# Expert stage of a hybrid diffusion step: the next chunk's first gate products between up and down, the result copied by ScalarE alone, one low weight piece on GpSimd

## The reference, cut to what matters

```python
xs = t[tok].astype(w_gate.dtype)                  # token rows, sorted by expert
hid = jax.nn.silu(lax.ragged_dot(xs, w_gate, sizes)) * lax.ragged_dot(xs, w_up, sizes)
y = lax.ragged_dot(hid, w_down, sizes)
```

## Time and profile before

| | us |
|---|---|
| median of three runs | 2013.52 |
| the three runs | 2010.44, 2013.52, 2013.54 |
| span of the profiled execution | 2009.7 |
| PE busy in it | 1754.8 (87%) |
| DVE busy | 1291.0 (64%) |
| ACT busy | 964.7 (48%) |
| POOL busy | 200.3 (10%) |

### The profile page before, as it was taken

The page is one execution under the profiler, slowest core; times in us unless marked ns, Lnnn a source line. Parts: engine busy times, 40 slices in busy tenths (PEclk is TensorE's granted clock), DMA queues, the critical chain, the costliest instruction groups (busy, mean ns, idle before and its releaser), DMA issues. The chain is left out here.

```text
span 2009.7 us, 40310 instructions
## 1 busy us (share of the span) xinstructions
PE 1754.8 (87%) x15365; PEld 1445.7 (72%) x15366; DVE 1291.0 (64%) x1849; ACT 964.7 (48%) x1499; POOL 200.3 (10%) x261
## 2 busy tenths in 40 slices
PE   3998977899897799999949998999998959999992
PEld 0898677788754688888838886888884548888882
DVE  1488354556545796896664872656664379899674
ACT  2254522333322786885544454323342257888651
POOL 0000022212100100000020000212220000000001
PEclk7999999999898899999969999999998969999996
DMA  8221094331023798897663111433002079999854
GB/s 323 73 85 45 1 363 166 129 128 54 6 114 153 311 393 355 319 399 279 235 220 115 43 45 42 142 128 97 2 3 108 32 295 383 400 404 396 334 209 167
DMA packets 113582, 376.64 MB, mean 187 GB/s; under 512 B 15178, under 2 KB 35938, under 8 KB 87846
## 3 DMA queue, kind: packets, MB, share of 16 engines
q1 hardware_dynamic: 84782, 303.86, 40.0%
q10 hardware_dynamic: 20168, 39.89, 5.1%
q0 software_dynamic: 8496, 30.94, 4.2%
HBM read 332.87 MB, written 41.78 MB: 186 GB/s over the span
## 5 line engine op out<-in xcount | busy, mean ns | idle before, releaser
L2084 DVE TENSOR_TENSOR expert_w_lo<-shared,expert_w_hi 128x2048 fp32r<-128x2048 f32 x192 | 430.4, 2284 | 46.6 <-ACT expert_w_hi L2026 45.7
L2026 ACT ACTIVATE expert_w_hi<-shared 128x2048 fp32r<-128x2048 f32 x192 | 359.6, 1909 | 44.0 <-PEq L143 39.6
L1968 PE MATMUL ps<-expert_w_hi,expert_x_hi 128*128 128x512 f32 x592 | 231.9, 392 | 6.3 <-DVE expert_x_lo L2080 6.3
L1970 PE MATMUL ps<-expert_w_hi,expert_x_lo 128*128 128x512 f32 x592 | 231.5, 391 | 0.0
L1969 PE MATMUL ps<-expert_w_lo,expert_x_hi 128*128 128x512 f32 x592 | 231.4, 391 | 0.0
L1968 PEld LDWEIGHTS ps<-expert_w_hi,expert_x_hi 128*128 128x128 f32 x592 | 111.9, 189 | 30.4 <-issue 7.1
L1970 PEld LDWEIGHTS ps<-expert_w_hi,expert_x_lo 128*128 128x128 f32 x592 | 111.8, 189 | 23.4
L1969 PEld LDWEIGHTS ps<-expert_w_lo,expert_x_hi 128*128 128x128 f32 x592 | 111.9, 189 | 23.2
L2004 PE MATMUL ps<-expert_w_hi,expert_hid_hi 128*128 128x512 f32 x296 | 118.6, 401 | 2.0 <-ACT expert_hid_hi L2058 1.1
L1127 POOL TENSOR_TENSOR mixer_NTb<-mixer_Bt,consts_sb 128x256 f32<-128x256 f32 x120 | 88.3, 758 | 285.5 <-DVE mixer_Bt L1402 222.2
L2005 PE MATMUL ps<-expert_w_lo,expert_hid_hi 128*128 128x512 f32 x296 | 115.5, 390 | 0.0
(11 more groups left out here) (372 smaller groups left out, 3668.1 us busy)
## 6 DMA issues: line engine op xcount, KB each, us to landing
shared<-in_w_up SPq DMA_DIRECT2D x64, 1024.0 KB, 8.6
shared<-in_w_down SPq DMA_DIRECT2D x64, 1024.0 KB, 8.9
shared<-in_w_gate SPq DMA_DIRECT2D x64, 1024.0 KB, 7.2
qkv<-in_w_ada SPq DMA_DIRECT2D x20, 1280.0 KB, 6.3
shared<-in_w_in SPq DMA_DIRECT2D x10, 2048.0 KB, 8.1
y_table<-expert_y ACTq DMA_DIRECT2D x37, 512.0 KB, 8.7
qkvT<-in_w_ada SPq DMA_DIRECT2D x20, 768.0 KB, 8.6
y_table<-zero ACTq DMA_DIRECT2D x1, 12800.0 KB, 52.3
```

Of the source, the lines that this page charges most:

```text
L1968: pe.matmul(bank, hi, w_hi[:, j, w], start=first, stop=False)
L1970: return pe.matmul(bank, lo, w_hi[:, j, w], start=False, stop=last)
L2026: act.activation(w_hi[:, j, :], raw[:, j, :], ACT.Copy).then_inc(w_hi_done, 1)
L2084: dve.tensor_tensor(w_lo[:, j, :], raw[:, j, :], w_hi[:, j, :].bitcast(F32), ALU.subtract).then_inc(w_lo_done, 1)
```

## The change

In `expert_phase` alone:

- TensorE: a chunk now consists of the second half of its gate products, the 8 transposes of the next x, the up products, the first half of the next chunk's gate products (`gate_head`) with the hid transposes behind its second and third product, and down. The first `gate_head` stands ahead of all chunks. In the very last chunk of a layer the next chunk's parts are left out, its x transposes too.
- x_hi and x_lo are made in halves of 128 x 512 (`x_half`).
- ScalarE: piece 0 of the next w_hi comes ahead of silu; the order is warm, piece 0, silu, piece 1, first half of x_hi, piece 2, second half of x_hi, the hid halves, pieces 3 and 4, y, piece 5, y transfer. y is one copy of 128 x 1024 out of banks 5 and 6.
- VectorE: piece 0, first half of x_lo, hid, second half of x_lo, the low parts of hid, pieces 1 to 4. It copies no y.
- GpSimd: makes the low part of piece 5 (`split_last`), behind the gather; gathers are numbered one higher and one is issued ahead of the chunks.
- SyncE: waits for piece 5 on a semaphore of its own (`w_lo_last`).

The diff, cut to its core:

```diff
                     for j in range(PIECES):
-                        sp.wait_ge(w_lo_done, e * PIECES + (j + 1))
+                        if j < LP:
+                            sp.wait_ge(w_lo_done, e * LP + (j + 1))
+                        else:
+                            sp.wait_ge(w_lo_last, e + 1)
                         sp.dma_start(raw[:, j, :], piece_of(A, l, e + 1, j)).then_inc(raw_in[j], 16)
...
-                def gather_next(k):
-                    pool.wait_ge(xt_p, k + 2)
+                def gather(k):
+                    pool.wait_ge(xt_p, k + 1)
                     pool.sem_inc(passed, 1)
-                    pool.tensor_copy(cur[:, :], R.idx[:, bass.ds(k + 1, 1)]).then_inc(picked, 1)
-                    pool.wait_ge(picked, k + 1)
+                    pool.tensor_copy(cur[:, :], R.idx[:, bass.ds(k, 1)]).then_inc(picked, 1)
+                    pool.wait_ge(picked, k)
...
-                for_experts(pool, lambda e, k, last, final: gather_next(k))
+                def split_last(e):
+                    pool.wait_ge(w_hi_done, e * PIECES + PIECES)
+                    pool.tensor_tensor(w_lo[:, LP, :], raw[:, LP, :], w_hi[:, LP, :].bitcast(F32), ALU.subtract).then_inc(w_lo_last, 1)
+
+                def chunk(e, k, last, final):
+                    if not (last and final):
+                        gather(nc.s_assert_within(k + 2, 2, MAXC))
+                        if last:
+                            split_last(e + 1)
+
+                gather(1)
+                split_last(0)
+                for_experts(pool, chunk)
...
-                def product(bank, hi, lo, j, col, first, last):
-
-                    w = slice(col, col + 512)
-                    pe.matmul(bank, hi, w_hi[:, j, w], start=first, stop=False)
-                    pe.matmul(bank, hi, w_lo[:, j, w], start=False, stop=False)
-                    return pe.matmul(bank, lo, w_hi[:, j, w], start=False, stop=last)
+                def product(bank, q, j):
+
+                    w, at = slice(q % 4 * FF, q % 4 * FF + 512), slice(q * P, (q + 1) * P)
+                    pe.matmul(bank, x_hi[:, at], w_hi[:, j, w], start=(q == 0), stop=False)
+                    pe.matmul(bank, x_hi[:, at], w_lo[:, j, w], start=False, stop=False)
+                    return pe.matmul(bank, x_lo[:, at], w_hi[:, j, w], start=False, stop=(q == KD - 1))
+
+                def gate(q):
+                    return product(G.ps[:, 0, :], q, q // 4)
+
+                def up(q):
+                    return product(G.ps[:, 1, :], q, 2 + q // 4)
+
+                def gate_head(e, k, between):
+
+                    pe.wait_ge(x_lo_done, k * 2 + 1)
+                    pe.wait_ge(w_lo_done, e * LP + 1)
+                    for q in range(4):
+                        mm = gate(q)
+                        if q in between:
+                            between[q]()
+                    mm.then_inc(g_half, 1)
 
                 for s in (u_p, xt_p, ht_p, y_p):
                     pe.sem_inc(s, 1)
-                turn(0, 0, KD)
+                turn(0)
+                gate_head(0, 0, {})
 
                 def chunk(e, k, last, final):
-                    pe.wait_ge(x_lo_done, k + 1)
+                    pe.wait_ge(x_lo_done, k * 2 + 2)
+                    pe.wait_ge(w_lo_done, e * LP + 2)
+                    for q in range(4, KD):
+                        mm = gate(q)
+                    mm.then_inc(g_p, 1)
+                    if not (last and final):
+                        turn(k + 1)
                     pe.wait_ge(hid_done, k * 2 + 1)
-                    for n, done in ((0, g_p), (1, u_p)):
-                        for q in range(KD):
-                            j = 2 * n + q // 4
-                            if q % 4 == 0:
-                                pe.wait_ge(w_lo_done, e * PIECES + (j + 1))
-                            at = slice(q * P, (q + 1) * P)
-                            mm = product(G.ps[:, n, :], x_hi[:, at], x_lo[:, at], j, q % 4 * FF, q == 0, q == KD - 1)
-                            if last and q == 3:
-                                mm.then_inc(half_used, 1)
-                        mm.then_inc(done, 1)
-                    turn(k + 1, 0, 4)
-                    hid_turn(k, 0)
-                    turn(k + 1, 4, 6)
-                    hid_turn(k, 1)
-                    turn(k + 1, 6, KD)
-                    pe.wait_ge(ya, k + 1)
-                    pe.wait_ge(yd, k + 1)
+                    for q in range(KD):
+                        if q % 4 == 0:
+                            pe.wait_ge(w_lo_done, e * LP + (3 + q // 4))
+                        mm = up(q)
+                        if q % 4 == 3:
+                            mm.then_inc((u_half, u_p)[q // 4], 1)
+                    if last and final:
+                        hid_turn(k, 0)
+                        hid_turn(k, 1)
+                    else:
+                        pe.wait_ge(sg_done, k + 1)
+                        gate_head(e + 1 if last else e, k + 1, {1: lambda: hid_turn(k, 0), 2: lambda: hid_turn(k, 1)})
+                    pe.wait_ge(y_done, k + 1)
                     for q in range(KF):
                         j, at = 4 + q // 2, slice(q * P, (q + 1) * P)
-                        if q % 2 == 0:
-                            pe.wait_ge(w_lo_done, e * PIECES + (j + 1))
+                        if q == 0:
+                            pe.wait_ge(w_lo_done, e * LP + LP)
+                        if q == 2:
+                            pe.wait_ge(w_lo_last, e + 1)
...
-                def take(k):
-                    act.wait_ge(xt_p, k + 2)
-                    act.wait_ge(u_p, k + 1)
-                    act.activation(x_hi[:, :], turned, ACT.Copy).then_inc(x_hi_done, 1)
+                def take(m):
+                    act.activation(x_hi[:, x_half(m)], turned[:, x_half(m)], ACT.Copy).then_inc(x_hi_done, 1)
 
...
                 split(0)
                 act.wait_ge(xt_p, 2)
-                act.activation(x_hi[:, :], turned, ACT.Copy).then_inc(x_hi_done, 1)
+                for m in range(2):
+                    take(m)
                 for j in range(1, PIECES):
                     split(j)
 
...
 
                         if last and not final:
                             act.wait_ge(raw_in[j], e * 16 + 16)
-                            if j % 2 == 0:
-                                act.wait_ge(half_used, e * 3 + (j // 2 + 1))
-                            elif j < 5:
-                                act.wait_ge((g_p, u_p)[j // 2], k + (1 + j // 2))
-                            else:
-                                act.wait_ge(y_p, k * 2 + 3)
+                            act.wait_ge((g_half, g_p, u_half, u_p, d_half, y_p)[j], k + (1, 1, 1, 2, 1, 2)[j])
                             split(j)
 
                     act.activation(warm[:, :], G.eps[:, :], ACT.Silu)
+                    next_hi(0)
                     act.wait_ge(g_p, k + 1)
                     act.wait_ge(hid_done, k * 2 + 1)
                     act.activation(sg[:, :], G.ps[:, 0, :], ACT.Silu).then_inc(sg_done, 1)
-                    for j in range(3):
-                        next_hi(j)
-                    act.wait_ge(y_p, k * 2 + 1)
+                    next_hi(1)
+                    if not (last and final):
+                        act.wait_ge(xt_p, k + 3)
+                        act.wait_ge(u_half, k + 1)
+                        take(0)
+                    next_hi(2)
+                    if not (last and final):
+                        act.wait_ge(u_p, k + 2)
+                        take(1)
+                    act.wait_ge(y_p, k + 1)
                     for m in range(2):
                         act.wait_ge(ht_p, k * 2 + (m + 2))
                         act.activation(h_hi[:, m * HQ * P:(m + 1) * HQ * P], hid_turned(m), ACT.Copy).then_inc(h_hi_done, 1)
-                    take(k + 1)
                     next_hi(3)
                     next_hi(4)
-                    act.wait_ge(y_p, k * 2 + 3)
+                    act.wait_ge(y_p, k + 2)
                     act.wait_ge(y_out, k * 16 + 16)
-                    act.activation(y[:, 0:512], G.ps[:, 5, :], ACT.Copy).then_inc(ya, 1)
+                    act.activation(y[:, :], G.ps[:, 5:7, :].rearrange("p b n -> p (b n)"), ACT.Copy).then_inc(y_done, 1)
                     next_hi(5)
-                    act.wait_ge(ya, k + 2)
-                    act.wait_ge(yd, k + 2)
+                    act.wait_ge(y_done, k + 2)
...
-                def take(k):
-                    dve.wait_ge(x_hi_done, k + 1)
-                    dve.tensor_tensor(x_lo[:, :], turned, x_hi[:, :].bitcast(F32), ALU.subtract).then_inc(x_lo_done, 1)
+                def take(k, m):
+                    dve.wait_ge(x_hi_done, k * 2 + (m + 1))
+                    dve.tensor_tensor(x_lo[:, x_half(m)], turned[:, x_half(m)], x_hi[:, x_half(m)].bitcast(F32),
+                                      ALU.subtract).then_inc(x_lo_done, 1)
 
...
```

(33 more changed lines are left out.)

22 lines of the change are left out of this document (12 added, 10 removed).

## The result

The changed kernel takes 2069.36 us (median of 4 runs, 2067.23 to 2078.41) where the kernel before takes 2011.98 (4 runs, 2008.63 to 2013.54): ratio 1.0295, 95% interval 1.0272 to 1.0318. Forecast: 2058, range 2036 to 2078, slower with 0.83.

What follows compares the result with a forecast made beforehand. TensorE, busy nearly throughout, bounds the kernel before; afterwards it waits for x_lo. Periods +34.7, chunk 0 +9.6 and tail +0.8 sum to +45 us on a 2009.7 us span: 2058 us on the median, range 2036 to 2078.

Steps and rivals of the forecast that it cites:

- other chunks: The 5 chunks not their expert's last, without weight splits: TensorE's work without waits, 17.65 us a period.
- Final chunks: The last chunk of each layer, which has no next chunk to prepare: 15.5 us.
- Behind other chunks: Four splitting chunks that follow a chunk not its expert's last and see no GpSimd split: 19.5 us.
- the circle: In-order chain from y copy through ScalarE's work, x_lo, gate head and down to the next P: 19.57 us.
- the table load follows 2.25 later: P+4.11: ScalarE's table load starts 2.25 us behind the end of the y DMA issue, 4.11 us behind P.
- P: Moment at which the matmul slot behind a chunk's last down product begins; periods run from one to the next.
- S is 11.45, the period 20.05: In splitting chunks the gate head starts (S) 11.45 us behind P, giving a period of 20.05 us.
- the turns: GpSimd's 4.54 us split and VectorE's instructions exclude each other, so VectorE's piece 0 runs P+8.4 to P+10.7.
- rival 1: GpSimd and VectorE overlap enough that the turns cost nothing: period 19.57, +28.5 us, 2042 us; chance 0.22.
- Chunk 0, +4.8 each: First chunk of each layer ends 4.8 us later, with VectorE's splits, GpSimd's and x_lo in sequence; twice, +9.6 us.
- Rival 3: TensorE's clock falls in its gap and the gate head doubles, +2.7 x 28 = +76 us, about 2134; chance 0.04.
- Rival 2: ScalarE comes in time, P to x_lo 9.0 us not 10.9: no TensorE gap, -30 us, about 1984; chance 0.13.

Runs made afterwards that it cites:

- on-chain copies: Changed kernel with two small 128x204 copies added on ScalarE ahead of its piece 1: 2112.99 us, ratio 1.0517 to the kernel before.
- Three edits: Changed kernel with piece 5's low part on VectorE, first x_hi half ahead of piece 1, y transfer issued by SyncE: 2004.07 us, 0.9971.

## Why the prediction was right, step by step

**Direction, place and size of the gap: right.** TensorE without waits was 17.65 a period: the other chunks take 17.78. Final chunks 15.5: 15.56. Behind other chunks 19.5: 19.69. TensorE idles 1.6 to 2.8 us ahead of the gate head, released by x_lo (2.4 was forecast); with chunk 0 its waits for x_lo are 74.2 us in all. The on-chain copies showed the circle to be real.

**"the table load follows 2.25 later: P+4.11": mis-sized.** It was taken from one row, and the row is typical of the kernel before: that stretch is 1.9 to 3.8 us there, median 2.26. I took it for a constant, and it is none: after the change it is 2.0 to 3.8, median 2.75, and 2.86 on the mean in split chunks, whose load comes at P+4.69. The term was 0.58 short. TensorE also restarts 0.15 behind x_lo, not 0.06, and gate head with down takes 8.78, not 8.60.

**"S is 11.45, the period 20.05": the sum near, the reason wrong.** I had the turns add 0.48 to ScalarE's 19.57. As the load comes late, GpSimd has finished (P+8.17) about when piece 0 is ready, and the turns add nothing. 19.57 + 0.58 + 0.09 + 0.18 = 20.42; measured 20.41. So the bound is ScalarE's circle alone, as rival 1 had it, only longer than rival 1 and I made it. That a turn of 0.48 which is not there stood in for most of the 0.85 that were missing is luck. On the size of a turn the step was right (4.54 forecast, 4.49 found, exclusive for a whole instruction), and rival 1's overlap does not exist; only the collision was missing.

**Chunk 0, +4.8 each: +6.1.** Now it splits: order +2.4, turn +2.15 (2.7 forecast), fall of the clock +1.55.

**Rival 3, at 0.04: it came in part.** "At the lower level the gate head alone doubles: +2.7 x 28" was wrong on both factors: 5 of 24 split gaps and both chunks 0, and 1.6 us each, since the lower level lay over a part of the gate head only: it began between 0.4 us ahead of it and 1.5 us into it, and was over by its end. That is 8.1 + 3.1 = 11 us. I had weighed, a window that kept its clock, too heavily: single windows do so here also.

**Rival 2, ScalarE in time:** it did not happen, for the reasons given. Three edits came close to its condition: they brought the end of x_lo from P+11.5 to P+9.4, where it asked for 9.0. That kernel beats the one before, by 6.6 us and not by 30: its 24 split periods are still 0.6 over 17.77 (14 us), and chunk 0 is 2.3 longer in each layer, which rival 2 had left out.

**The sum for the profiled execution.** Split periods 24 x (20.41 - 20.05) = 8.6, clock 8.1, the other periods 1.5: 18.2, against 18.1 between 678.5 and 696.6. Chunk 0 adds 2.7 to its forecast, and +2.1 ahead, -0.7 between and -0.3 at the tail make 22: the span was forecast at 2054.8 and is 2076.7. On the medians the miss is 11 us.

**Open.** Why the stretch behind the transfer's issue varies and grew, and why of gaps of like length some bring the clock down (1.97 us did, 2.80 did not), no run tells. Low-clock periods differ between executions, so a difference of 5 us between two of these kernels is no more than their number.

## What to carry to other kernels

Moving a consumer earlier moves the deadline of all that feeds it: walk the feeder's in-order chain from one period to the next and close the circle before counting what is won. Where two limits are nearly equal, undoing one shows nothing; undo both before acquitting either. Ask of each wait that is moved to another engine what is queued behind it there, and keep the instruction that brings the table load first.

## What the runs showed of the hardware

- The transfer of y, issued on ScalarE with the wait for the y copy ahead of it, delayed ScalarE's next instruction by 1.1 to 2.0 us (table load at P+4.20 to 5.11, against P+3.13 in every split chunk once another engine issued it).
- The same transfer issued by GpSimd landed 9.1 us behind its issue, with 373 GB/s moved in all. The program waits there for the landing, and GpSimd's next instruction came 11.4 us behind the issue.
- Waits of TensorE of 1.80 us (the run with the y transfer on SyncE and piece 5 on GpSimd) and of 1.97 us (the kernel after) were enough to bring the clock from 2.4 to 1.2 GHz behind them; with sixteen transposes in the gap, none of 48 did. The Trainium skill (TensorE: Matmul & The Clock Gate, HAM oscillation) warns of idle gaps between bursts, of longer ones than these. The runs agree on the gaps and show that short ones can do it too, though not every one does.
- VectorE and GpSimd, both reading two operands in SBUF, took strict turns: 5.00 us for an instruction of 2.29, 6.12 for one of 4.49 (the kernel after, chunk 0).
